# Two w_ada column groups multiplied in fp32 without a split, the input projection begun on its first four k blocks, sampled states turned later, and the last residual additions moved to VectorE

## What is computed

```
mod = silu(c) @ w_ada + b_ada                  # c: 9 rows (8 sampled, 1 prompt); w_ada: 1024 x 6144
sh1, s1, g1, sh2, s2, g2 = split(mod, 6)       # 1024 columns each
h   = rmsnorm(x) * norm1_g * (1 + s1) + sh1    # 520 rows
z   = h @ w_in                                 # w_in: 1024 x 6144; feeds three mixers and their gates
...                                            # conv (31 taps), pooling, short conv, merge, w_o
x   = x + g1 * m
h   = rmsnorm(x) * norm2_g * (1 + s2) + sh2
x   = x + g2 * moe(h)                          # 16 experts, 2 per token
y   = rmsnorm(x) * final_g
```

## Time and profile before

| | us |
|---|---|
| median of 3 runs | 923.63 (920.33 to 923.87) |
| profiled execution, its own time | 920.84 |
| its span | 919.1 |
| PE busy | 810.4 (88%) |
| DVE busy | 706.6 (77%) |
| ACT busy | 480.5 (52%) |
| POOL busy | 59.6 (6%) |
| mean granted TensorE clock | 0.936 of full speed |

### The profile page before, as it was taken

The page is one execution under the profiler, slowest core; times in us unless marked ns, Lnnn a source line. Parts: engine busy times, 40 slices in busy tenths (PEclk is TensorE's granted clock), DMA queues, the critical chain, the costliest instruction groups (busy, mean ns, idle before and its releaser), DMA issues.

```text
span 919.1 us, 14726 instructions
## 1 busy us (share of the span) xinstructions
PE 810.4 (88%) x4942; PEld 696.8 (76%) x4942; DVE 706.6 (77%) x942; ACT 480.5 (52%) x559; POOL 59.6 (6%) x62
## 2 busy tenths in 40 slices
PE   4679999999999999999998369999999999999800
PEld 2469899889889899899776257888888888888600
DVE  4782438878778998598358749899999989998658
ACT  5752433343432321632223237888888888888532
POOL 0002000000000000230000000000100000010062
PEclk9679999999999999999999569999999999999955
DMA  9855645455445432123832179988897899999352
GB/s 307 263 166 173 239 151 161 138 160 161 161 138 177 133 111 69 53 80 127 262 111 88 52 257 340 380 326 310 324 370 252 324 401 399 396 398 402 123 208 93
DMA packets 91117, 201.88 MB, mean 220 GB/s; under 512 B 8781, under 2 KB 13389, under 8 KB 91030
## 3 DMA queue, kind: packets, MB, share of 16 engines
q1 hardware_dynamic: 78865, 165.45, 51.5%
q0 software_dynamic: 4960, 17.89, 5.4%
q10 hardware_dynamic: 7247, 17.94, 5.3%
HBM read 183.07 MB, written 18.91 MB: 220 GB/s over the span
## 4 chain that ended last, share of the span: by engine, by line
PE 80%; DVE 10%; ACT 3%; issue 3%; DMA 2%; POOL 2%; SPq 1%; ACTq 0%; POOLq 0%; DVEq 0%
PE ps L664 31%; PE ps L561 13%; PE ps L563 13%; PE ps L562 13%; PE ps L741 3%; DVE w_lo L1299 2%; PE ps L823 2%; PE ps L694 1%; DMA region_a<-in_x_sample_dram 1%; ACT w_hi L915 1%; PE ps L589 1%; POOL region_b L1257 1%; PE ps L590 1%; PE ps L794 1%; PE ps L850 1%
## 5 line engine op out<-in xcount | busy, mean ns | idle before, releaser
L1299 DVE TENSOR_TENSOR w_lo<-raw,w_hi 128x1024 fp32r<-128x1024 f32 x220 | 263.2, 1223 | 116.1 <-ACT w_hi L915 107.4
L915 ACT ACTIVATE w_hi<-raw 128x1024 fp32r<-128x1024 f32 x220 | 226.5, 1057 | 217.3 <-PE ps L664 158.5
L561 PE MATMUL ps<-w_hi,hT_hi 128*128 128x512 f32 (+1 forms) x512 | 206.5, 403 | 6.4 <-DVE hT_lo L1299 5.6
L563 PE MATMUL ps<-w_hi,hT_lo 128*128 128x512 f32 (+1 forms) x512 | 203.4, 397 | 0.0
L562 PE MATMUL ps<-w_lo,hT_hi 128*128 128x512 f32 (+1 forms) x512 | 203.3, 397 | 0.0
L664 PE MATMUL ps<-hT_hi,w_hi 128*128 128x260 f32 x768 | 156.6, 285 | 3.7 <-DVE hT_lo L1299 3.6
L664 PE MATMUL ps<-hT_lo,w_hi 128*128 128x260 f32 x768 | 155.0, 283 | 0.0
L664 PE MATMUL ps<-hT_hi,w_lo 128*128 128x260 f32 x768 | 154.8, 283 | 0.0
L664 PEld LDWEIGHTS ps<-hT_hi,w_hi 128*128 128x128 f32 x768 | 118.7, 189 | 7.9 <-DVE w_lo L1299 3.9
L664 PEld LDWEIGHTS ps<-hT_lo,w_hi 128*128 128x128 f32 x768 | 119.4, 190 | 0.0
L664 PEld LDWEIGHTS ps<-hT_hi,w_lo 128*128 128x128 f32 x768 | 118.8, 189 | 0.0
(11 more groups left out here) (277 smaller groups left out, 749.1 us busy)
## 6 DMA issues: line engine op xcount, KB each, us to landing
raw<-in_exp_w_dram SPq DMA_DIRECT2D x96, 512.0 KB
region_a<-in_exp_w_dram SPq DMA_DIRECT2D x80, 512.0 KB
raw<-in_w_ada_dram SPq DMA_DIRECT2D x48, 512.0 KB
raw<-in_w_in_dram SPq DMA_DIRECT2D x48, 512.0 KB
expert_rows<-region_b ACTq DMA_DIRECT2D x18, 512.0 KB, 6.5
region_b<-in_exp_w_dram SPq DMA_DIRECT2D x16, 512.0 KB
expert_rows<-region_a POOLq DMA_DIRECT2D x8, 512.0 KB, 7.8
raw<-in_w_o_dram SPq DMA_DIRECT2D x8, 512.0 KB
```

The costliest lines, as they stand in the source:

```text
L561: pe.matmul(out, pairs[0], moving[0], start=start, stop=False)
L563: return pe.matmul(out, pairs[1], moving[0], start=False, stop=stop)
L915: act.activation(w_hi[:, split_slot(n), :], place, ACT.Copy).then_inc(hi_done, 1)
L1299: return dve.tensor_tensor(out, whole, first.bitcast(F32), ALU.subtract)
```

## The change

- The two w_ada groups of the shift (G_NAT = 2) leave `ITEMS`. Their eight quarters are loaded to eight places of their own (`nat_place`), in front of everything, with x between the fourth and the fifth. TensorE multiplies them in fp32 as they are (`native_group`, 8 products of 16 by 512 columns per group), without `hi` and `lo`. N_HEAD is 8, N_MIX 88.
- The bias rows and the parameter rows are issued from ScalarE's queue. The rows of conf and pool states are issued by SyncE ahead of split quarter 12.
- Squares start tile by tile as x lands. Mean, root and scaling are ahead of the first `lo`.
- `turn_params` keeps the parameters, the short-conv state and the sampled x. The conf and pool states are turned at the first three a groups between z groups (`turn_states`), and copied out there (`states_out`).
- Shift and scale columns are turned in two steps, groups 0 to 2 and then group 3, the latter inside the first z quarter into bank 6. `scale_out`, `sampled_input` and `sampled_rest` work on halves. The first z group can begin when k blocks 0 to 3 have their scale; set 3 of its first quarter waits for the second half.
- The last additions of all tiles are made on VectorE, each behind its g2 product. GpSimd only gathers.

```diff
+G_NAT = 2
 G_HEAD = 4
-ITEMS = [("a", g) for g in range(G_HEAD)] + [("z", 0), ("z", 1)]
+ITEMS = [("a", g) for g in range(G_NAT, G_HEAD)] + [("z", 0), ("z", 1)]
-N_HEAD = 4 * G_HEAD
+N_HEAD = 4 * (G_HEAD - G_NAT)
...
+            for h in range(4):
+                native(h)
+            for i in range(NP // P):
+                sp.dma_start(x_in[:, i, :], x_prompt[0, i * P:(i + 1) * P, :]).then_inc(x_landed[i], 16)
+            sp.dma_start(x_in[0:ND, 4, :], x_sample.rearrange("b t d -> (b t) d")).then_inc(x_landed[4], 16)
+            for h in range(4, 4 * G_NAT):
+                native(h)
...
+            def native_group(g):
+                for q in range(4):
+                    pe.wait_ge(nat_ready[4 * g + q], 16)
+                    w = nat_place[4 * g + q].rearrange("p (k n) -> p k n", k=2)
+                    for k in range(2):
+                        kk = 2 * q + k
+                        m = pe.matmul(ps[0:16, 5 + g, :], c_pad[:, kk, :], w[:, k, :], start=(kk == 0), stop=(kk == KD - 1))
+                m.then_inc(nat_used, 1)
...
+            pe.wait_ge(turned_out, 1)
+            for g in range(G_NAT):
+                native_group(g)
+            pe.wait_ge(xn_ready, NTILE)
+            for k in range(4):
+                turn_x(k, k)
...
+            pe.wait_ge(mod_ready, 1)
+            ada_quarter(0, 5)
+            ada_quarter(1, 5)
+            for k in range(4, KD):
+                if k > 4:
+                    pe.wait_ge(xT_out, k - 4)
+                turn_x(k, (4, 0, 1, 2)[k - 4])
+            ada_quarter(2, 5)
+            ada_quarter(3, 5)
+            pe.wait_ge(xT_out, KD)
+            turn_params()
+            ada_quarter(4, 7)
+            ada_quarter(5, 7)
+            for g in range(3):
+                t = turn_mod(g, 0, 36 * g)
             t.then_inc(modT_done, 1)
+            ada_quarter(6, 7)
+            ada_quarter(7, 7)
...
-                        if m == 2 and ITEMS[n // 4 - 1][0] == "a":
+                        if m == 2 and g == 0:
+                            turn_mod(3, 6, 0).then_inc(modT_done, 1)
+                        elif m == 2 and ITEMS[n // 4 - 1][0] == "a":
                             pe.wait_ge(mod_ready, ITEMS[n // 4 - 1][1] + 1)
+                        elif m == 3 and g == 0:
+                            pe.wait_ge(scaleT_ready, 2)
...
+            act.dma_start(mod, b_ada[0, 0:2 * D].partition_broadcast(ND + 1)).then_inc(ld_mod, 16)
             act.wait_ge(ld_c, 32)
             act.activation(c_raw[0:ND + 1, :], c_raw[0:ND + 1, :], ACT.Silu).then_inc(silu_c_ready, 1)
+            for dst, src in row_loads:
+                act.dma_start(dst, src).then_inc(ld_rows, 16)
...
+            input_sampled(0)
+            input_prompt(0)
+            input_prompt(1)
+            hi(7)
+            hi(8)
...
+            dve.wait_ge(ld_mod, 16)
+            mod_group(0)
+            mean_squares()
+            norm_root()
+            for t in range(NTILE):
+                dve.tensor_scalar(x_in[0:rows(t), t, :], x_in[0:rows(t), t, :], sums[0:rows(t), 3, t:t + 1], None, ALU.mult).then_inc(xn_ready, 1)
+            mod_group(1)
+            for n in range(5):
+                lo(n)
+            params_out()
+            mod_group(2)
+            lo(5)
+            lo(6)
+            scale_out(0)
+            sampled_input(0)
+            prompt_sum(0)
+            prompt_sum(1)
+            sampled_rest(0)
+            prompt_rest(0)
+            lo(7)
+            lo(8)
+            mod_group(3)
+            prompt_rest(1)
+            for k in range(2, 4):
+                prompt_sum(k)
+                prompt_rest(k)
+            lo(9)
+            scale_out(1)
+            sampled_input(1)
+            prompt_sum(4)
+            sampled_rest(1)
+            prompt_rest(4)
...
-                if i >= 3:
-                    for t in ((0,) if i == 3 else range(1, NTILE - 1)):
-                        pool.wait_ge(moe_ready, t + 1)
-                        pool.tensor_tensor(x1[0:rows(t), t, :], x1[0:rows(t), t, :], yg[t % 4][0:rows(t), 1, :], ALU.add).then_inc(x2_ready, 1)
...
+                    link(dve.tensor_tensor(y[0:n, 1, :], y[0:n, 1, :], g2, ALU.mult), moe_ready, i + 1)
+                    dve.tensor_tensor(x1[0:n, i, :], x1[0:n, i, :], y[0:n, 1, :], ALU.add).then_inc(x2_ready, 1)
```

More of the change, by code:

```diff
@@ L60 @@
 ITEMS += [("z", _g) for _g in range(2 + G_ADA - G_HEAD, G_IN)]
[L61 removed]
+A_AT = {g: ITEMS.index(("a", g)) for g in range(G_NAT, G_ADA)}
 Z_AT = [ITEMS.index(("z", g)) for g in range(G_IN)]
[L63 removed]
+N_HEAD = 4 * (G_HEAD - G_NAT)
 N_MIX = 4 * len(ITEMS)
@@ L255, in trunk_step @@
         ld_x = sem("ld_x")
+        x_landed = [sem(f"x_landed{i}") for i in range(NTILE)]
+        nat_ready = [sem(f"nat_ready{h}") for h in range(4 * G_NAT)]
+        nat_used = sem("nat_used")
+        ld_states = sem("ld_states")
         ld_rows = sem("ld_rows")
@@ L668, in z_quarter @@
                 mm.then_inc(quarter_used, 1)
-            for i in range(G_HEAD, len(ITEMS)):
+            for i in range(G_HEAD - G_NAT, len(ITEMS)):
                 kind, g = ITEMS[i]
@@ L945, in _, with input_sampled @@
[L945 to L949, removed]
-                act.activation(hT_hi[:, k, 0:NP], xnT[:, k, :], ACT.Identity, bias=shiftT[:, k, ND:ND + 1], scale=scaleT[:, k, ND:ND + 1]).then_inc(hT_hi_done, 1)
+            def input_sampled(half):
+                act.wait_ge(scaleT_ready, half + 1)
+                act.wait_ge(hT_raw, half + 1)
+                ks = slice(4 * half, 4 * half + 4)
+                act.activation(hT_hi[:, ks, NP:NT], dec_in[:, ks, :], ACT.Copy).then_inc(hT_hi_done, 1)
@@ new lines, in input_prompt @@
+            def input_prompt(k):
+                act.activation(hT_hi[:, k, 0:NP], xnT[:, k, :], ACT.Identity, bias=shiftT[:, k, ND:ND + 1], scale=scaleT[:, k, ND:ND + 1]).then_inc(hT_hi_done, 1)
+            hi(0)
+            hi(1)
+            for k in range(4):
+                turned_x(k)
+            hi(2)
+            hi(3)
+            for k in range(4, KD):
+                turned_x(k)
+            hi(4)
+            hi(5)
+            hi(6)
+            act.wait_ge(xT_out, KD)
+            input_sampled(0)
@@ L951, in _ @@
+            input_prompt(0)
+            input_prompt(1)
+            hi(7)
+            hi(8)
+            input_prompt(2)
+            input_prompt(3)
+            hi(9)
+            input_sampled(1)
+            for k in range(4, KD):
+                input_prompt(k)
+            hi(10)
+            hi(11)
             for n in range(N_HEAD + 4, N_HEAD + 7):
@@ L1371, in prompt_rest @@
                 dve.wait_ge(hT_sum, k + 1)
[L1372 removed]
+                dve.wait_ge(hT_hi_done, k + 2 + k // 4)
                 rest(hT_lo[:, k, 0:NP], (tmp_a, tmp_b)[k % 2][:, 0:NP], hT_hi[:, k, 0:NP]).then_inc(hT_lo_done, 1)
[L1375 to L1389 removed]
@@ L1390, in _ @@
-            lo(N_HEAD)
-            lo(N_HEAD + 1)
-            mod_group(G_HEAD - 1)
-            lo(N_HEAD + 2)
-            scale_out()
-            sampled_input()
-            sampled_rest()
-            for k in range(KD + 1):
-                if k < KD:
-                    prompt_sum(k)
-                if k:
-                    prompt_rest(k - 1)
-                if k == 3:
-                    lo(N_HEAD + 3)
+            dve.wait_ge(ld_mod, 16)
+            mod_group(0)
+            mean_squares()
@@ new lines, in _ @@
+            prompt_rest(0)
[12 more added lines that the diff above has]
+            prompt_rest(4)
+            for k in range(5, KD):
+                prompt_sum(k)
+                prompt_rest(k)
+            lo(10)
+            lo(11)
```

185 lines of the change are left out of this document (83 added, 102 removed).

## The result

Median of four executions after the change: 913.24 us (911.73 to 913.76); before, 922.53 (920.33 to 923.87). The ratio is 0.9908, 95% interval 0.9889 to 0.9926: faster by 0.9%. The forecast was 914.0. The profiled execution's own time is 911.73 us with a span of 909.6, against 920.84 and 919.1.

What follows compares the result with a forecast made beforehand. TensorE was taken to bound the kernel from 59.85 us, except at its two ends. Terms -6.1 + 1.3 - 3.4 = -8.2 us gave 912.6 from the profiled time and 915.4 from the median; the middle, 914.0, was forecast, range 909 to 919.

Steps and rivals of the forecast that it cites:

- Head: Kernel start through the first z group: projection starts at 52.7 us, group ends at 78.7 against 84.8, so -6.1 us.
- The charge of 4.2 us for the small loads: Loads at the start: bias, parameter rows and states delay the large loads by 4.2 us, between 0 and 6.2.
- The stay of 26 us: First z group of the projection: lasts 26 us, from 52.7 to 78.7, longer than 24.94 by what it waits for.
- States: State transposes between z groups: 12 in three lots come into a TensorE-bound stretch, 0.45 us a lot, +1.3 us.
- End: Last additions moved to VectorE: 7.6 us of slow instructions go, 5.0 are added; last product at 913.4 against 916.84, -3.4.
- two sums: Whole kernel: -8.2 us gives 912.6 from the profiled execution's time and 915.4 from the median; the middle is 914.0.
- (1): First projection group: waits keep TensorE at 1.2 GHz throughout, 20 us more, time 930.6; chance 0.04.
- (2): Head: no charge for small loads, second unsplit group from 17.2, all behind 4 us earlier, time 910.0; chance 0.14.
- (3): Second unsplit group in the head: lower clock throughout, ends at 35.3, all behind 4.9 us later, 918.9; chance 0.14.
- (4): First z group: VectorE's list comes 3 to 4 us late, sets wait, the earlier start is lost, 917; chance 0.10.
- (5): Kernel end: VectorE additions cost 5.0 us and only as much of the slow instructions goes, 917.4; chance 0.10.

Runs made afterwards that it cites:

- run 3: The changed kernel with the eight small parameter-row loads issued on SyncE's queue behind the sixth split quarter: 910.45 us, ratio 0.9880 to the kernel before.
- run 7: The changed kernel with the load of 31 conv-tap rows given as two loads, of 16 and 15 rows: 908.88 us, ratio 0.9873 to the kernel before.
- run 9: The changed kernel with conv taps in two loads and the splits of quarters 7 and 8 issued ahead: 903.33 us, ratio 0.9809 to the kernel before.
- run 10: run 9's kernel with the second half of the scale, `scale_out(1)`, ahead of `lo(9)`: 904.08 us, ratio 0.9811 to the kernel before.
- run 1: The changed kernel with the last additions back on GpSimd, its head as changed: 916.96 us, ratio 0.9947 to the kernel before.
- run 8: The changed kernel without the 12 conv and pooling state transposes, their places set to zero: 912.7 us in one execution.
- run 11: The changed kernel measured once more, unedited, on the chip of run 10: 913.18 us, ratio 0.9915 to the kernel before.
- run 2: The kernel before with only the last additions moved to VectorE: 918.63 us, ratio 0.9962 to the kernel before.
- run 4: The changed kernel with four more fp32 products, results unused, between the two unsplit groups: 910.24 us, ratio 0.9874 to the kernel before.
- run 5: The changed kernel with the splits of quarters 7 and 8 issued ahead of the input's first pieces: 907.09 us, ratio 0.9850 to the kernel before.

## Why the prediction was right

**Head, -6.1 forecast.** The order of events held, and nearly every time in it: unsplit group 1 to 30.4 (30.3), x scaled at 27.1 (27.1), turned columns to 45.6 (45.7), first `hT_hi` 47.2 (47.0), `lo(8)` to 52.2 (51.9), projection 52.7 (52.5), wait until 54.9 (54.8), `scale_out(1)` to 59.3 (58.7). Two estimates erred against each other under that: quarter 4 at 21.4 came at 20.3, and the group then took 10.0 us, not 9.0. The charge of 4.2 us for the small loads was 2.9 by run 3, of which 1.3 to 2.0 are the shape of one load (runs 7, 9 and 10).

The term that was mis-sized is "The stay of 26 us": the first group took 25.2, from 52.51 to 77.75. A group is 192 products, so 48 a quarter and 24 for each k block. Three quarters of 5.8 us were right; the first quarter had 8.6 us (52.7 to 61.3) and took 8.0, because the clock rose one microsecond behind the start and not 3.6 us behind it, as before. So the head gave 7.2 in this execution, by the end of the second group. In the three other traces with this head (runs 1, 8 and 11) the pair of groups takes 50.3 to 50.6 us, 2.0 to 2.4 longer, which makes -5: the forecast lies between the two, and the execution with the trace is the favourable one.

**States, +1.3 forecast, 0 measured** (after against before, and run 8). I had put 12 transposes "into a TensorE-bound stretch" without asking whether it is that inside: at the start of each w_ada group TensorE is ahead of the splits.

**End, -3.4 forecast, -3.6 measured** (-3.7 in run 2, 0 in run 1). Walked instruction by instruction, and right by instruction.

**Not foreseen:** 1.3 us in the router, from where the clock falls in one execution. The errors are -1.1, -1.3 and -0.2 against +1.3, and the sum was off by 1.3 in the span (-8.2 against -9.5) and by 0.9 in own time (-9.1). The median moved by 9.3 us; 914.0 was 0.8 high. That it is so close is in part luck: the three errors of the terms lie on one side and make 2.6 us, half of which the router took back, with a cause that no term had. And 914.0 is the middle of two sums, 912.6 and 915.4; from the medians alone the sum would have been 2.2 high.

**Rivals.** (1) came true in a tenth of its size: the clock stays low for 1 to 8 us of the first group, not for all of it, and costs up to 2.4 of the 20 us. (2) was reached only by edits (runs 3, 4, 7: 909 to 910.5); its 17.2 for quarter 4 is the 17.4 of run 3. (3) did not appear; group 1 took 8.7 to 10.0 us in five executions with the same loads, not the 13.9 of this rival. (4) is refuted: one wait of 0.91 us in the group, where it was expected. (5) is refuted by runs 1 and 2.

## What to carry to other kernels

Before you charge work to a stretch that TensorE "bounds", look for waits inside that stretch: small work placed just ahead of a wait is free. The hole in front of a group can cost twice, once as idle time and once as the lower clock behind it, so filling a hole of 3.6 us, even with products whose result nobody uses, saved 3.0 us of the group behind it (run 4). And look at the shape of the small loads that run beside the large ones, and at what a split that everybody waits for is queued behind: two such edits of a few lines (run 9) gave as much as the whole change had.

## What the runs showed of the hardware

- A load of 31 rows, 62 KB, issued beside loads of 512 KB, has these land 1.3 to 2.0 us later than two loads of 16 and 15 rows do, at the same total GB/s (382 and 384); the last 2 KB packet of its queue starts at 17.5 us and not at 11.9.
- A group of eight fp32 products of 512 columns takes 7.0 us at the full clock (0.88 each); behind idle times of 3.6 to 5.0 us it took 10.0, 9.9, 9.5, 8.7 and 8.7 us (after and runs 1, 11, 5 and 8), behind 0.9 to 3.0 us (runs 3, 4, 7, 9 and 10) always 7.0. Within either range a longer hole did not make a longer group.
- From one execution to the next the rise of the granted clock in the first projection group moves by up to 6.5 us (53.6 in after, 60.1 in run 1), and its fall in the router moves too (16 products in 2.27, 2.79, 2.99, 3.31 or 3.60 us): a scatter of 1 to 2 us each, of the size of the differences between executions of one kernel.
- An addition on GpSimd (2.47 us; VectorE's takes 1.22) holds one VectorE instruction with two tensors to read until it is over: the 128x1 L1599 takes 1.92 and 2.13 us beside it and 0.22 elsewhere, 0.94 on average. A reciprocal with one tensor to read keeps its 0.16 us (trace of before, 896 and 902 us).
